# An encoder's first projection as rounded products, their low weight parts summed by accumulating transfers

## The reference

```python
def conv_module(h, w_pw1, b_pw1, w_dw, b_dw, ln_g, ln_b, w_pw2, b_pw2):
    u = h @ w_pw1 + b_pw1                      # (256, 2048) @ (2048, 4096)
    a, gate = jnp.split(u, 2, axis=-1)
    v = a * jax.nn.sigmoid(gate)
    v = depthwise_conv(v, w_dw) + b_dw         # causal, 31 taps, per channel
    v = jax.nn.silu(layernorm(v, ln_g, ln_b))
    return v @ w_pw2 + b_pw2
...
h = x
y = rmsnorm(h, attn_norm_g[0])
h = h + conv_module(y, ...)
h = h + swiglu(rmsnorm(h, ffn_norm_g[0]), ...)
...
```

## Time and profile before

| | |
|---|---|
| time, median of 3 runs (lowest, highest) | 2124.07 us (2123.8, 2124.23) |
| the profiled execution | 2124.01 us, its span 2122.2 us |
| mean granted TensorE clock | 0.997 |
| PE busy | 2082.7 us, 98% of the span |
| DVE busy | 1284.3 us, 61% |
| ACT busy | 790.8 us, 37% |
| POOL busy | 20.8 us, 1% |
| DMA | 374.91 MB, mean 177 GB/s |

### The profile page before, as it was taken

How to read it: one execution, slowest core, us unless ns; L and a number is a source line. 1 busy time by engine, 2 the same in 40 slices (tenths; PEclk the granted TensorE clock), 3 DMA queues, 4 the chain that set the end, 5 groups by cost and what they waited for, 6 DMA issues and landing times.

```text
span 2122.2 us, 25267 instructions
## 1 busy us (share of the span) xinstructions
PE 2082.7 (98%) x9810; PEld 1747.1 (82%) x9810; DVE 1284.3 (61%) x1568; ACT 790.8 (37%) x727; POOL 20.8 (1%) x23
## 2 busy tenths in 40 slices
PE   6999999999999999999999999999999999999997
PEld 6888878888888888888888888888888888888886
DVE  2999986555555555555566665465555555555555
ACT  3000263433333333333344444353333333333343
POOL 0000000000000000000001000000000000000001
PEclk9999999999999999999999999999999999999999
DMA  6444446555556555565545434656556555565551
GB/s 205 158 146 152 139 156 204 192 186 196 182 194 195 183 195 185 191 198 182 194 139 149 139 119 146 210 180 197 182 189 201 182 195 185 190 198 182 194 191 67
DMA packets 219728, 374.91 MB, mean 177 GB/s; under 512 B 17180, under 2 KB 58916, under 8 KB 219172
## 3 DMA queue, kind: packets, MB, share of 16 engines
q1 hardware_dynamic: 218256, 370.76, 53.9%
q10 hardware_dynamic: 1428, 3.55, 0.5%
HBM read 372.18 MB, written 2.10 MB: 176 GB/s over the span
## 4 chain that ended last, share of the span: by engine, by line
PE 94%; DVE 3%; ACT 1%; issue 1%; DMA 0%; SPq 0%; DVEq 0%; ACTq 0%
PE ps L1139 90%; DVE scratch L803 2%; PE ps L1291 1%; PE ps L1473 1%; PE ps L1472 1%; DMA scratch<-in_conv_b_dw_dram 0%; PE ps L1453 0%; PE ps L1183 0%; PE ps L1172 0%; DVE resid L967 0%; ACT scratch L635 0%; ACT w_hi L435 0%; PE ps L1454 0%; DVE x_lo L724 0%; SPq L318 0%
## 5 line engine op out<-in xcount | busy, mean ns | idle before, releaser
L697 DVE TENSOR_TENSOR w_lo<-raw,w_hi 128x2048 fp32r<-128x2048 f32 x321 | 734.8, 2292 | 605.3 <-ACT w_hi L435 604.4
L435 ACT ACTIVATE w_hi<-raw 128x2048 fp32r<-128x2048 f32 x321 | 614.2, 1918 | 876.5 <-PE ps L1139 863.1
L1139 PE MATMUL ps<-w_hi,x_hi 128*128 128x512 f32 x1728 | 675.2, 391 | 1.4 <-DVE x_lo L724 1.0
L1139 PE MATMUL ps<-w_hi,x_lo 128*128 128x512 f32 x1728 | 672.7, 389 | 0.0
L1139 PE MATMUL ps<-w_lo,x_hi 128*128 128x512 f32 x1728 | 672.3, 389 | 0.0
L1139 PEld LDWEIGHTS ps<-w_hi,x_hi 128*128 128x128 f32 x1728 | 324.4, 188 | 69.3 <-DVE x_lo L724 1.5
L1139 PEld LDWEIGHTS ps<-w_hi,x_lo 128*128 128x128 f32 x1728 | 324.4, 188 | 67.6
L1139 PEld LDWEIGHTS ps<-w_lo,x_hi 128*128 128x128 f32 x1728 | 324.5, 188 | 66.5
L1139 PE MATMUL ps<-w_hi,a_hi 128*128 128x512 f32 (+1 forms) x768 | 292.3, 381 | 2.4 <-DVE a_lo L944 2.4
L1139 PE MATMUL ps<-w_hi,a_lo 128*128 128x512 f32 (+1 forms) x768 | 292.0, 380 | 0.0
L1139 PE MATMUL ps<-w_lo,a_hi 128*128 128x512 f32 (+1 forms) x768 | 292.0, 380 | 0.0
(11 more groups left out here) (175 smaller groups left out, 888.3 us busy)
## 6 DMA issues: line engine op xcount, KB each, us to landing
raw<-in_ffn_w_gate_dram SPq DMA_DIRECT2D x88, 1024.0 KB
raw<-in_ffn_w_up_dram SPq DMA_DIRECT2D x88, 1024.0 KB
raw<-in_ffn_w_down_dram SPq DMA_DIRECT2D x88, 1024.0 KB
raw<-in_conv_w_pw_dram SPq DMA_DIRECT2D x64, 512.0 KB
raw<-in_conv_w_pw_dram SPq DMA_DIRECT2D x16, 1024.0 KB
raw<-in_mla_w_o_dram SPq DMA_DIRECT2D x16, 1024.0 KB
raw<-in_mla_w_ukv_dram SPq DMA_DIRECT2D x8, 1024.0 KB
raw<-in_mla_w_dq_dram SPq DMA_DIRECT2D x4, 1024.0 KB
```

Of the source, the lines that this page charges most:

```text
L435: act.activation(w_hi[:, slot, :], raw[:, slot, :], ACT.Copy).then_inc(hi_done, 1)
L697: dve.tensor_tensor(w_lo[:, g % RING, :], raw[:, g % RING, :], hi32(w_hi[:, g % RING, :]), ALU.subtract).then_inc(lo_dve, 1)
L1139: ins = pe.matmul(dst, lhsT, rhs, start=first and n == 0, stop=last and n == len(pairs) - 1, skip_group_check=skip)
```

## The change

1. **Three rounded products.** The first projection uses `w_hi`, `w_lo`, `x_hi` and `x_lo` like all the others. `halves(False, ...)` does the two products with `w_hi`, `halves(True, ...)` the one with `w_lo`; in each pass all 16 positions of the group. `x_f` is gone; the start does `chunk_hi` and `chunk_lo` for all 16 tiles, with `hi` and `lo` of groups 0 to 3 between them.
2. **Accumulating transfers.** For groups 4 to 35 (`ACC0` to `ACC1`: the rest of the first projection, and the first four groups of the second) DVE's subtraction is replaced. `hi_and_negative` on ACT writes `w_hi` from `raw`, and then minus the rounded value to `w_lo`, as a second copy of `raw` with scale -1. POOL then issues a transfer that adds `raw` to `w_lo` in place, one per group, counted by `lo_acc` of the slot. TensorE, and the load that reuses the slot of `raw`, wait for `lo_acc`.
3. **Two taps of each tile as diagonal products.** In eighths 0 to 6, taps 0 and 1 go to TensorE (8 products in `conv_rows(s)`), and DVE does 29; ACT makes the diagonals. `acc` is then added by four products with the identity instead of being transposed. The last eighth keeps 14 and 17. DVE's wait for `conv_tr` moves ahead of its write to `vbuf`, which TensorE now reads.

```diff
-PE_TAPS_LAST = 14
-DVE_STEPS = 2 * TAPS
+PE_TAPS = [2] * (HALVES - 1) + [14]
+CONV_STEPS = [1 + sum(2 * (TAPS - PE_TAPS[r]) for r in range(s)) for s in range(HALVES + 1)]
+ACC0, ACC1 = G_PW1 + KG, G_PW2 + RING
...
         def wait_lo(eng, g, i=None, per=0):
-            eng.wait_ge(lo_dve, val(g - G_PW2 + 1, i, per))
+            if ACC0 <= g < ACC1:
+                eng.wait_ge(lo_acc[g % RING], 16 * ((g - ACC0) // RING + 1))
+            else:
+                eng.wait_ge(lo_dve, val(g + 1 if g < ACC0 else g - (ACC1 - ACC0) + 1, i, per))
...
                     if g >= RING:
-                        sp.wait_ge(group_used, g - RING + 1)
+                        wait_lo(sp, g - RING)
...
+            for g in range(ACC0, ACC1):
+                slot = g % RING
+                pool.wait_ge(neg_done, g - ACC0 + 1)
+                pool.dma_start(hi32(w_lo[:, slot, :]), raw[:, slot, :], accum_op=ALU.add).then_inc(lo_acc[slot], 16)
...
+            def hi_and_negative(g):
+                slot = g % RING
+                hi(g)
+                act.activation(w_lo[:, slot, :], raw[:, slot, :], ACT.Copy, scale=-1.0).then_inc(neg_done, 1)
...
+                hi(G_PW1)
                 act.wait_ge(rstd_ready, 1)
...
+            for n in range(CC):
+                chunk_hi(0, n, R_ATTN)
+                if n < KG - 1:
+                    hi(G_PW1 + n + 1)
...
+            diagonals(0)
+            for s in range(HALVES):
+                g = G_PW1 + KG * (s + 1)
+                hi_and_negative(g)
+                if s >= 2:
+                    rows_out(s - 2)
+                    diagonals(s - 1)
+                if s < HALVES - 1:
+                    diagonals(HALVES - 1, 4 * s, 4 * s + 4)
+                hi_and_negative(g + 1)
+                hi_and_negative(g + 2)
                 gate_sigmoid(s)
+                hi_and_negative(g + 3)
...
+                for n in range(CC):
+                    chunk_lo(0, n, gain)
+                    lo(G_PW1 + n)
...
             def conv_half(s):
-                w0 = 0 if s < HALVES - 1 else PE_TAPS_LAST
+                w0 = PE_TAPS[s]
                 dve.wait_ge(group_used, G_PW1 + KG * s + KG)
+                if s >= 2:
+                    dve.wait_ge(conv_tr, TT * (s - 1))
...
-                            ins = product(ps[:, 2 * u + m // 2, S * (m % 2):S * (m % 2) + S],
-                                          [(w[:, kk, P * m:P * m + P], x_f[:, k, :])],
...
+                                pairs = [(wl[:, kk, cols], x_hi[:, k, :])] if low else \
+                                    [(wh[:, kk, cols], x_hi[:, k, :]), (wh[:, kk, cols], x_lo[:, k, :])]
...
+                    if s == 0:
+                        pe.wait_ge(hi_done, g + 1)
+                        pe.wait_ge(xlo_done, GK * (j + 1))
+                    else:
+                        wait_lo(pe, g)
                     if s >= 2 and j == 0:
                         pe.wait_ge(glu_done, 2 * (s - 1))
+                    halves(False, True, False)
+                    if s == 0:
+                        wait_lo(pe, g)
+                    halves(True, False, True).then_inc(group_used, 1)
...
             def conv_rows(s):
+                for mm in range(2):
+                    pe.wait_ge(glu_done, 2 * s + mm + 1)
+                    for w in range(PE_TAPS[s]):
+                        for t in range(TT):
+                            product(ps[:, 4 + 2 * u + t, P * mm:P * mm + P],
+                                    [(vbuf[:, 2 * u + mm, w + P * t:w + P * t + P], diag_of(s, mm, w))],
+                                    mm == 0 and w == 0, False, skip=True)
+                pe.wait_ge(conv_step, CONV_STEPS[s + 1])
                 for t in range(TT):
                     for mm in range(2):
-                        ins = pe.transpose(ps[:, 4 + 2 * u + t, P * mm:P * mm + P], acc[:, 2 * u + mm, P * t:P * t + P],
-                                           ident[:, :])
+                        ins = product(ps[:, 4 + 2 * u + t, P * mm:P * mm + P],
+                                      [(acc[:, 2 * u + mm, P * t:P * t + P], ident[:, :])], False, True, skip=True)
```

More of the change, by code:

```diff
@@ L202, in encoder @@
         hi_done = sem("hi_done")
+        neg_done = sem("neg_done")
+        lo_acc = [sem(f"lo_acc{n}") for n in range(RING)]
         lo_dve = sem("lo_dve")
@@ L330, in square_loads @@
                         load(tile_rows(w, slice(GK * j, GK * j + GK), bass.ds(i * CH + CH, CH)), g0 + KG + j, i, KG)
-            square_loads(conv_w_pw2[0], G_PW2)
+            for n in range(CC):
+                for j in range(KG):
+                    load(tile_rows(conv_w_pw2[0], slice(GK * j, GK * j + GK), slice(CH * n, CH * n + CH)), G_PW2 + KG * n + j)
             def ffn_loads(l, g0):
@@ L448, in first_norm @@
                 act.wait_ge(vec_done, 1)
[L449 to L453, removed]
             def chunk_hi(norm, n, gain):
@@ L471, in _, with diagonals @@
             first_norm(R_ATTN)
+            for n in range(CC):
+                chunk_hi(0, n, R_ATTN)
+                if n < KG - 1:
+                    hi(G_PW1 + n + 1)
             act.wait_ge(vec_done, 3)
[L473 to L476, removed]
+            def diagonals(s, lo_=0, hi_=2 * PE_TAPS[0]):
+                for n in range(lo_, hi_):
+                    mm, w = n // PE_TAPS[s], n % PE_TAPS[s]
+                    act.activation(diag_of(s, mm, w), ident[:, :], ACT.Copy,
+                                   scale=tap_col[:, w, 2 * s + mm:2 * s + mm + 1]).then_inc(diag_done, 1)
             def gate_sigmoid(s):
@@ L1207, in channel_half, with halves @@
                     g = G_PW1 + KG * s + j
-                    pe.wait_ge(raw_in[g % RING], LANDED * (g // RING + 1))
-                    w = w_rows(raw, g % RING)
+                    wh, wl = w_rows(w_hi, g % RING), w_rows(w_lo, g % RING)
+                    def halves(low, first, last):
+                        for kk in range(GK):
+                            k = GK * j + kk
+                            for m in range(CM):
+                                cols = slice(P * m, P * m + P)
+                                pairs = [(wl[:, kk, cols], x_hi[:, k, :])] if low else \
+                                    [(wh[:, kk, cols], x_hi[:, k, :]), (wh[:, kk, cols], x_lo[:, k, :])]
+                                ins = product(ps[:, 2 * u + m // 2, S * (m % 2):S * (m % 2) + S], pairs,
+                                              first and k == 0 and m % 2 == 0, last and k == KT - 1, skip=True)
+                        return ins
@@ L1253, in _ @@
             conv_rows(HALVES - 2)
-            conv_rows_last()
+            conv_rows(HALVES - 1)
             pe.wait_ge(row_done, TT * HALVES)
```

64 lines of the change are left out of this document (11 added, 53 removed).

## The result

| | before | after |
|---|---|---|
| median, 4 runs each (lowest, highest) | 2124.15 us (2123.8, 2124.63) | 2149.62 us (2147.77, 2151.05) |
| span of the profiled execution | 2122.2 us | 2148.0 us |
| DMA | 374.91 MB | 408.55 MB |

The ratio of after to before is 1.0119, with an interval of 1.0102 to 1.0137. The forecast was 2103 us and faster; 2149.6 lies inside the range of 2100 to 2175, on the wrong side of the kernel before. That the range holds it is owed to its width, not to the mechanism forecast. The span grew by 25.8 us.

What follows compares the result with a forecast made beforehand. TensorE was taken to bound the kernel: first eighth -4.8 us, the other seven -18.3, first sums +2, tail +0.4, together -20.7, from 2124.0 to 2103 us; the range of 8 in 10 was 2100 to 2175.

Steps and rivals of the forecast that it cites:

- TensorE's products and `conv_rows`: First projection on TensorE: products fall to 23.04 us an eighth, `conv_rows` grows from 0.60 to 2.73, together 25.77.
- DVE: Convolution taps on DVE: four fewer an eighth take 1.59 us off, 25.94 to 24.35, staying under TensorE's 25.77.
- Start, first sums and tail: Ends of the first projection: first eighth -4.8 us, short time for first sums +2, last eighth's tail +0.4.
- The accumulating transfer: POOL's 1 MB add into `w_lo`: price not in the trace, between 2.37 and 7.1 us, taken as hidden.
- I take it to be hidden: Accumulating transfers in the first projection cost no time beside TensorE's 25.77 us an eighth; chance 0.45, 2099 to 2108 us.
- 11.85 + 4a: DMA engines' us an eighth: 11.85 for four loads, plus four accumulating transfers of a us each.
- The price of a load: Weight loads of 1 KB rows at 354 GB/s: 2.96 us for 1 MB, four an eighth 11.85 us.
- The first rival: DMA engines become the bound: transfer costs two reads, 4.74 us, an eighth 30.8, total 2138 us; chance 0.27.
- Slow adding: Accumulating transfers take 7.1 us each, 40.3 us an eighth, TensorE waits in every group: 2205 us; chance 0.15.
- Issuing blocks DVE: POOL's preparing of 32 transfers holds up DVE's taps; at 1.1 us each the gain is gone, about 2124; chance 0.08.
- ACT's order: A `hi` waiting for a late load ahead of the sigmoid costs 1 to 2 us an eighth: 2113; chance 0.05.
- a falling clock: Sign that the prediction fails altogether: a granted clock below 1.00 in the first projection's eighths.

Runs made afterwards that it cites:

- the mended mixture: Changed kernel with every fourth group subtracted by DVE instead of summed by transfer, group 35's subtraction moved into the SiLU steps: 2115.91 us, ratio 0.9964.

## Why the prediction was wrong, point by point

- **TensorE's products and `conv_rows`: right.** 25.77 us an eighth counted, 25.71 measured once no transfer was in the way. Moving the taps adds 2.24 us, 2.13 counted.
- **DVE: right.** Taps 0.397 us each beside 32 issues on POOL. Without transfers its work on an eighth takes 24.4 us (95.45 to 119.82), 24.35 counted, and it then waits 1.34 us, within the 0.9 to 1.4 counted.
- **Start, first sums and tail: nearly right.** The first eighth ends at 46.78 without transfers and 47.37 with them; 46.5 was counted. Without transfers the tail took 2097.6 - 223.40 = 1874.2 us, 0.7 less than before, where 0.4 more was counted. The first sums, put at 2 us, do not show as a term of their own: the second eighth of the changed kernel takes 31.0 us, 6.0 over its 23.04 and these 2, and each later one is 6.7 over on average.
- **The accumulating transfer: this step failed**, in the sentence "I take it to be hidden". The sum above it, 11.85 + 4a, had 25.77 us an eighth reached at a = 3.5 and 28.07 at a = 4.05; a is 5.23. To be hidden at that price, the transfers would have had to run in time that the loads' share already counts as busy, and no run shows such room beyond a sum of 1.05 to 1.07 over 140 us. The figures of two queues add: 40.6 and 53.9% with copies, where all was hidden; 82.7 and 16.4% with quarter loads, where TensorE still never rested in that window; 66.6 and 38.3% in the changed kernel, where it waited. The shares of 1.06 and 1.08 in 2 us had shown that limit, not free room above it.
- **The price of a load: a little small.** It was put at 2.96 us, from 354 GB/s in a window whose share was 1.08. Rows 8 had it: a share of 0.48 at 151 GB/s is 3.33 us for 1 MB, and 3.22 are measured beside the transfers.
- **The first rival was the right mechanism, and its size a little small.** It had 30.8 us an eighth and 2138. (The first of its seven eighths was forecast at 23.04 us, so its own figures give 2141.) Divided by the share of 1.05, a transfer takes 5.23 / 1.05 = 5.0 us, not 4.74, and a load 3.22 / 1.05 = 3.07, not 2.96: four of each are 32.2 us. The rival's reason, two reads for one write, fits the ratio of 5.23 to a copy's 2.65, and about half the price for half the width. No run separates the reads from the adding, so that the second read is the cause is argued, not shown. By the rule of the Trainium skill, "Collectives: The Full Stack", section "The bandwidth ceiling: the fold count and why AG ≠ RS ≠ AR", an add in a transfer runs at half a copy's rate; the measured 1.97 to 1 agrees, here outside a collective.
- **Slow adding (7.1 us): refuted.** An add of 1 MB takes 5.0 to 5.5 us of the engines in every run that has one.
- **Issuing blocks DVE: refuted.** An issue takes POOL 0.86 us, and the taps beside it are not longer. The rule that the prediction names for it is about GpSimd instructions that read SBUF, and no run shows an issue to be one.
- **ACT's order: not a cause.** ACT does wait for loads, 106.2 us, but with copies in place of sums the same order gives 2100.43 us.

The chance of 0.27 on the right rival against 0.45 on hiding was the error of judgement. The deciding 4.05 us lay between the two bounds of the price, 2.37 and 7.1; two reads at the copy's rate were the mechanism at hand, and at 4.74 they lay above it.

## What to carry to other kernels

Before calling a transfer hidden, add up the busy shares of all queues in that stage, the new one's included, and hold the sum against 1: engine time per transfer is share times window over the number of transfers, and an accumulating one cost about twice a copy here (5.23 us for 2.65). A landing time that grows, as from 5 to 18 us here, while the engine time of a load stays (3.35 and 3.22 us), is a queue, not a slow transfer. Where one kind of work has two possible places and either alone is overfull (here the DMA engines with four groups in four, DVE with four in four), split it, and leave the part without cover, such as the last eighth, out of the split: 2115.9 us, against 2149.6 and 2157.8 for the extremes.

## What the hardware showed that was not expected

**POOL and DVE take turns**, as in the timelines above: 4.9 us when POOL holds the field, 13 to 22 us beside taps in the rows of 60 to 275 us. The Trainium skill, "SBUF — State Buffer", section "Who interferes with whom", calls the port pair that the two share an exclusive lock; the rows agree. The issue of a transfer on POOL shows nothing of it.

**The granted clock falls after a wait.** After TensorE's wait of 3.47 us ahead of 111.38, windows of 3 us show (columns as above):

```profile
108.00:111.00 3.00, 0.00 (x0) 0.00 (x0) 0.00 (x0) 3.00 (x2) 0.86 (x1) 1.00 0.97 199
112.00:115.00 3.00, 3.00 (x16) 3.00 (x16) 2.92 (x8) 3.00 (x3) 0.75 (x1) 0.50 1.14 183
116.00:119.00 3.00, 3.00 (x28) 3.00 (x27) 3.00 (x8) 0.00 (x0) 0.86 (x1) 1.00 1.11 299
```

0.50 is 1.2 GHz, and products then start 0.21 us apart instead of 0.12. I had named a falling clock as what would fail the prediction altogether; here it follows from the waits. The seven eighths take 226.0 us for 176.6 without transfers (46.78 to 223.40). Of these 49.4 us TensorE waits 30.0; the other 19 go with a mean clock of 0.92 in that stretch. The DMA engines set the pace all the same: TensorE's work at full clock, 25.71 us, leaves 6.8 us an eighth to spare, and where the share is as full but the clock stands at 0.99, in the mended mixture, the engines' sum again gives the eighths.
